# The first two weight tiles of each MLP, computed token-major in a four-layer hybrid trunk

## What is computed

```python
def rmsnorm(x, g):
    y = xf * lax.rsqrt(jnp.mean(xf * xf, axis=-1, keepdims=True) + NORM_EPS)
    return (y * g.astype(jnp.float32)).astype(x.dtype)

def sq_relu_mlp(h, w1, w2):
    a = jax.nn.relu(h @ w1)
    return (a * a) @ w2

x = x + sq_relu_mlp(rmsnorm(x, norm_mlp[i]), mlp_w1[i], mlp_w2[i])
```

## Time and profile before

| | |
|---|---|
| runs of before | 1424.39, 1426.0, 1428.05 us; median 1426.0 us |
| span of the profiled execution | 1423.9 us |
| PE busy | 1357.3 us, 95% of the span |
| DVE, ACT busy | 858.0 us (60%), 667.9 us (47%) |
| mean granted PE clock | 0.981 of full speed |
| DMA | 162 GB/s on average |

### The profile page before, as it was taken

How to read it: one execution, slowest core, us unless ns; L and a number is a source line. 1 busy time by engine, 2 the same in 40 slices (tenths; PEclk the granted TensorE clock), 3 DMA queues, 4 the chain that set the end, 5 groups by cost and what they waited for, 6 DMA issues and landing times.

```text
span 1423.9 us, 20299 instructions
## 1 busy us (share of the span) xinstructions
PE 1357.3 (95%) x8600; PEld 1212.8 (85%) x8600; DVE 858.0 (60%) x1125; ACT 667.9 (47%) x834; POOL 40.3 (3%) x58
## 2 busy tenths in 40 slices
PE   5999989999999899999998999999999999899997
PEld 5788779999899799998897988999988787799996
DVE  4676565555554565555897786655555766565553
ACT  3454444444354454443665554544434454454442
POOL 2000000000000000000101110000000000000000
PEclk9899999999999999999998999999998999999999
DMA  7653246655565275552773444665626143375540
GB/s 235 173 145 119 89 163 214 199 178 178 151 175 178 93 248 185 198 182 89 231 231 114 149 149 133 221 196 192 190 60 237 54 137 99 103 236 189 196 149 30
DMA packets 147834, 231.06 MB, mean 162 GB/s; under 512 B 7651, under 2 KB 116493, under 8 KB 147744
## 3 DMA queue, kind: packets, MB, share of 16 engines
q1 hardware_dynamic: 144896, 221.66, 47.5%
q0 software_dynamic: 2848, 8.10, 2.7%
HBM read 227.08 MB, written 2.65 MB: 161 GB/s over the span
## 4 chain that ended last, share of the span: by engine, by line
PE 85%; DVE 8%; ACT 3%; issue 2%; DMA 2%; POOL 0%; SPq 0%; DVEq 0%; POOLq 0%; ACTq 0%
PE bank L501 14%; PE bank L503 14%; PE bank L502 14%; PE acc L696 11%; PE acc L695 11%; PE acc L699 11%; PE bank L829 4%; DVE wlo L484 3%; ACT whi L474 2%; PE bank L847 1%; PE bank L837 1%; DMA raw<-in_mla_w_in 1%; PE bank L630 1%; DMA raw<-in_mla_w_ukv 1%; PE bank L1270 1%
## 5 line engine op out<-in xcount | busy, mean ns | idle before, releaser
L484 DVE TENSOR_TENSOR wlo<-raw,whi 128x2048 fp32r<-128x2048 f32 (+2 forms) x209 | 467.5, 2246 | 208.0 <-ACT whi L474 207.9
L474 ACT ACTIVATE whi<-raw 128x2048 fp32r<-128x2048 f32 (+2 forms) x209 | 388.7, 1870 | 94.1 <-PE acc L699 82.9
L501 PE MATMUL bank<-hhi,whi 128*128 128x256 f32 x1448 | 415.7, 287 | 11.1 <-DVE hlo L574 7.1
L502 PE MATMUL bank<-hlo,whi 128*128 128x256 f32 x1448 | 411.8, 284 | 0.0
L503 PE MATMUL bank<-hhi,wlo 128*128 128x256 f32 x1448 | 411.8, 284 | 0.0
L501 PEld LDWEIGHTS bank<-hhi,whi 128*128 128x128 f32 x1448 | 278.8, 193 | 17.3 <-DVE hlo L574 9.0
L502 PEld LDWEIGHTS bank<-hlo,whi 128*128 128x128 f32 x1448 | 279.0, 193 | 3.3 <-issue 1.0
L503 PEld LDWEIGHTS bank<-hhi,wlo 128*128 128x128 f32 x1448 | 278.9, 193 | 0.2
L696 PE MATMUL acc<-wlo,uhi 128*128 128x512 f32 x512 | 200.0, 391 | 0.0
L695 PE MATMUL acc<-whi,uhi 128*128 128x512 f32 x512 | 199.6, 390 | 0.0
L699 PE MATMUL acc<-whi,ulo 128*128 128x512 f32 x512 | 159.1, 389 | 0.0
(11 more groups left out here) (212 smaller groups left out, 1678.2 us busy)
## 6 DMA issues: line engine op xcount, KB each, us to landing
raw<-in_mlp_w SPq DMA_DIRECT2D x128, 1024.0 KB, 5.3
raw<-in_ssd_w_in SPq DMA_DIRECT2D x18, 1024.0 KB, 6.2
raw<-in_mla_w_o SPq DMA_DIRECT2D x16, 1024.0 KB, 4.9
raw<-in_mla_w_ukv SPq DMA_DIRECT2D x8, 1024.0 KB, 7.4
raw<-in_moba_w_qkv SPq DMA_DIRECT2D x16, 512.0 KB, 6.1
raw<-in_ssd_w_out SPq DMA_DIRECT2D x8, 1024.0 KB, 5.0
raw<-in_mla_w_uq SPq DMA_DIRECT2D x8, 768.0 KB, 6.4
raw<-in_mla_w_in SPq DMA_DIRECT2D x4, 1024.0 KB, 9.1
```

What stands on the lines that cost most here:

```text
L474: nc.scalar.activation(whi[:, s, :e], raw[:, s, :e], ACT.Copy).then_inc(w_hi_done[s], 1)
L484: nc.vector.tensor_tensor(wlo[:, s, :e], raw[:, s, :e], whi[:, s, :e].bitcast(F32), ALU.subtract).then_inc(w_split[s], 1)
L501: nc.tensor.matmul(ps, lhs[0], rhs[0], start=start, stop=False)
L502: nc.tensor.matmul(ps, lhs[0], rhs[1], start=False, stop=False)
```

## The change

The products of up 0 and up 1 are taken the other way round: the turned input of one token tile is stationary (128 tokens) and 256 weight columns move. The four pieces (token tile t, unit c) are `rows(t, c)`, 24 matmuls each, and the result of a tile, 128 tokens by 512 hidden channels, stands in one PSUM bank. Relu and square are taken in that layout. Then `turn(t)` turns the squares of a tile with four transposes into a bank, from which ACT and DVE make `uhi` and `ulo`. PE's order becomes rows(0,0), the eight transposes of tile 1, rows(0,1), rows(1,0), rows(1,1), turn(0), up 2, turn(1), down 0, down 1, up 3, down 2 and on as before. DVE scales both halves of tile 1 before it makes any of tile 1's `hlo`. ACT and DVE split up 2 between the two tiles' relus and squares, and down 1 between the two tiles' `uhi` and `ulo`.

```diff
@@ plan_mlp
+                if c == 1:
+                    jobs.add(("rows", L, 0))
+                    jobs.add(("rows", L, 1), ready=used(("up", L, 1)))
+                    jobs.add(("uT", L, 0), freed=(ulo_done, mlp_base[L] + 1))
+                elif 2 <= c < NCH:
                     jobs.add(("up", L, c), ready=used(("up", L, c)))
+                    if c == 2:
+                        jobs.add(("uT", L, 1), freed=(ulo_done, mlp_base[L] + 2))
@@ dve_norm, deferred
-                dve_tr(dve, j, 1, [0])
                 dve_scale_half(dve, j, 1, 1)
-                dve_tr(dve, j, 1, [1])
+                dve_tr(dve, j, 1)
@@ pe_mlp
             def down(c, tiles=range(T)):
-                te.wait_ge(ulo_done, mlp_base[L] + c + 1)
+                te.wait_ge(ulo_done, mlp_base[L] + max(c + 1, T))
                 pe_out(te, ("down", L, c), hidden(c), c == 0, False, tiles)

-            pe_first_channels(te, j, [("up", L, 0), ("up", L, 1)])
+            def rows(t, c):
+                wait_unit(te, ("up", L, c))
+                ps = open_job(te, ("rows", L, t)) if c == 0 else bank[jobs.at["rows", L, t][0]]
+                w = hi_lo(("up", L, c))
+                for k in range(KD):
+                    mm = mm3(ps[:, c * CH:(c + 1) * CH], (hhi[:, k, tok(t)], hlo[:, k, tok(t)]),
+                             (w[0][:, k, :], w[1][:, k, :]), k == 0, k == KD - 1)
+                if t == T - 1:
+                    mm.then_inc(used(("up", L, c))[0], 1)
+                elif c == 1:
+                    mm.then_inc(ready(("rows", L, t)), 1)
+
+            def turn(t):
+                te.wait_ge(usq_done, mlp_base[L] + t + 1)
+                ps = open_job(te, ("uT", L, t))
+                for b in range(4):
+                    mm = nc.tensor.transpose(ps[:, b * P:(b + 1) * P], rsq[:, t, b * P:(b + 1) * P], ident[:])
+                mm.then_inc(ready(("uT", L, t)), 1)
+
+            tile_ready(te, j, 0)
+            rows(0, 0)
+            pe_tr(te, j, 1)
+            rows(0, 1)
+            tile_ready(te, j, 1)
+            rows(1, 0)
+            rows(1, 1)
+            turn(0)
+            wait_unit(te, ("up", L, 2))
+            pe_channels(te, open_job(te, ("up", L, 2)), ("up", L, 2), CH)
+            turn(1)
             for c in range(2, NCH):
                 down(c - 2, [0] if c == NCH - 1 else range(T))
-                wait_unit(te, ("up", L, c))
-                pe_channels(te, open_job(te, ("up", L, c)), ("up", L, c), CH)
+                if c > 2:
+                    wait_unit(te, ("up", L, c))
+                    pe_channels(te, open_job(te, ("up", L, c)), ("up", L, c), CH)
@@ act_mlp
-            for c in range(NCH):
+            for t in range(T):
+                act_splits(act, ("up", L, 0), AHEAD - 1 + t)
+                ps = job_ready(act, ("rows", L, t))
+                nc.scalar.activation(relu[:, t, :], ps[:], ACT.Relu).then_inc(freed(("rows", L, t)), 1)
+            for t in range(T):
+                ps = job_ready(act, ("uT", L, t))
+                nc.scalar.activation(turned(uhi, t), ps[:].rearrange("p (b n) -> p b n", b=4),
+                                     ACT.Copy).then_inc(uhi_done, 1)
+                if t == 0:
+                    act_splits(act, ("down", L, 0), AHEAD - 1)
+            for c in range(2, NCH):
@@ dve_mlp
-            for c in range(NCH):
+            for t in range(T):
+                dve_splits(dve, ("up", L, 0), AHEAD - 1 + t)
+                job_copied(dve, ("rows", L, t))
+                nc.vector.tensor_tensor(rsq[:, t, :], relu[:, t, :], relu[:, t, :], ALU.mult).then_inc(usq_done, 1)
+            dve_square_rstd(dve, j)
+            for t in range(T):
+                dve.wait_ge(uhi_done, mlp_base[L] + t + 1)
+                nc.vector.tensor_tensor(turned(ulo, t), bank[jobs.at["uT", L, t][0]][:].rearrange("p (b n) -> p b n", b=4),
+                                        turned(uhi, t).bitcast(F32), ALU.subtract).then_inc(ulo_done, 1)
+                if t == 0:
+                    dve_splits(dve, ("down", L, 0), AHEAD - 1)
+            for c in range(2, NCH):
```

More of the change, by code:

```diff
@@ L294, in plan_mlp @@
                     unit(("up", L, c), KD, CH, cols(w1, c * CH, (c + 1) * CH))
+                if c == 1:
[3 more added lines that the diff above has]
+                elif 2 <= c < NCH:
                     jobs.add(("up", L, c), ready=used(("up", L, c)))
+                    if c == 2:
+                        jobs.add(("uT", L, 1), freed=(ulo_done, mlp_base[L] + 2))
                 if c >= 1:
                     unit(("down", L, c - 1), 2, DM, rows(w2, (c - 1) * CH, c * CH))
+        mlp_base, n_mlp = {}, 0
+        for kind, L, i in stages:
+            if kind == "mlp":
+                mlp_base[L] = NCH * n_mlp
+                n_mlp += 1
         step_unit = {}
@@ L766, in mlp_splits, with turned @@
         def mlp_splits(splits, eng, L, c):
[L768 to L771, removed]
+            splits(eng, ("down", L, c - 1), AHEAD - 1 if c < NCH - 1 else 1)
+        def turned(hidden, t):
+            return hidden[:, :, :, tok(t)].rearrange("p c i n -> p (c i) n")
         def act_mlp(act, j, L):
-            for c in range(NCH):
+            for t in range(T):
[9 more added lines that the diff above has]
+            for c in range(2, NCH):
                 mlp_splits(act_splits, act, L, c)
@@ L796, in dve_mlp @@
                                         ALU.subtract).then_inc(ulo_done, 1)
-                if c == 0:
-                    dve_square_rstd(dve, j)
             dve_splits(dve, ("down", L, NCH - 1), AHEAD - 1)
[L801 to L805, removed]
         def pe_attn(te, j, L, heads, qk, qk_waits, v_of, v_waits, piece):
```

## The result

The changed kernel took **1428.18 us** (median of 20 runs, 1424.23 to 1431.22), the one before 1424.51 us (20 runs beside them). The ratio is **1.0025, 95% interval 1.0016 to 1.0033**: 3.7 us slower, a difference that 20 runs each can show, and just under the 0.3% that the prediction took as its bound. One run of before beside experiments 1 to 4, 2227.2 us at a granted clock of 0.556, was in a slower state and is left out throughout.

What follows compares the result with a forecast made beforehand. PE, 85% of the span, bounds the kernel. Per MLP +0.88 +1.30 +1.67 -2.43, less 0.16, is +1.26 us, four times +5.0: span 1428.9, plus 2.1 to the runs' median, 1431.0 us; range 1427.0 to 1435.5.

Steps and rivals of the forecast that it cites:

- The saving at the front: At each MLP's entry, PE's old waits for tile 1's `xn` and `hlo` and small pieces go: 2.43 us saved per MLP.
- Turned operands at no cost: In up 0 and up 1, 96 matmuls of 256 columns before and after, still 0.12 us each with the weights moving.
- The transposes: turn(0) and turn(1) add eight transposes in PE's queue: 0.88 us per MLP, 3.5 us in all.
- The wait for up 2's weights: PE ahead of up 2 waits for DVE's split of its weights: 1.30 us per MLP, none before.
- The wait for `ulo`: Between turn(1) and down 0 PE waits for ACT's copy and DVE's rest: 2.03 us, 1.67 of it beside the transposes.
- The stretch: From the old stage's last matmul to the start of down 1: 27.3 us instead of 26.03, 1.26 us later per MLP.
- The clock: One fall of the granted clock still expected among the four MLP entries, as before, so 4 x 1.26 = +5.0 us.
- Rival (a): The third MLP's clock fall goes: +3.5, 1429.5 us; if the fourth's goes too, +2.0, 1428.0; chance 27 in 100.
- my own sum: The main forecast over four MLP entries: +5.0 us, 1431.0 us, its own range 1429.5 to 1432.5; 45 in 100.
- Rival (b): The clock falls two to four more times behind new idle with transposes, 1.5 us each: 1434.0 to 1437.0 us; chance 17.
- Rival (c): Not slower: DVE ends up 2's split by 201.01, so no wait there; 1425.8 us, or 1424.3; chance 7 in 100.
- Rival (d): PE still stands at tile 1's transposes or rows(1,0), old waits stay: +8.7 us more, 1439.7 us; chance 4 in 100.

Runs made afterwards that it cites:

- Experiment 1: Changed kernel with turn(1) placed between the two halves of up 2 instead of behind it; 1422.34 us, ratio to before 0.9986.
- experiment 2: Changed kernel with ACT's two sums of squares moved from ahead of down 0's split to behind up 2's split; 1424.77 us, ratio to before 1.0006.
- experiment 3: Changed kernel with turn(1) in the middle of up 2 and ACT's sums of squares behind up 2's split; 1416.01 us, ratio to before 0.9939.
- experiment 4: Changed kernel with each group of four transposes of squares issued twice, same values written twice; 1429.38 us, ratio to before 1.0026.
- Experiment 6: Changed kernel with DVE's old order, first half of tile 1's `hlo` ahead of scaling its second half; 1442.04 us, ratio to before 1.0133.
- experiment 7: Kernel before with only ACT's two sums of squares moved behind down 0's split; 1424.09 us, ratio to before 1.0003.
- experiment 5: Changed kernel with tile 1's eight transposes ahead of rows(0,0) instead of behind it; 1428.66 us, ratio to before 1.0031.

## Why the prediction was right

**The saving at the front: right.** 2.43 us of waits per MLP were to go, and no idle is left between the old stage's last matmul and turn(0). The two slacks claimed for `xn` and `hlo` were there: 1.26 us (`xn` scaled at 188.44, turned from 189.70) and about 1.1 (the second `hlo` done at 192.26, rows(1,0) due at 193.4). Experiment 6 shows that the first depends wholly on DVE's new order.

**Turned operands at no cost: right.** 72 matmuls in 8.7 us is 0.12 us each, as with the input moving.

**The transposes: right in price.** Eight more per MLP; four take 0.36 us, and 0.44 when something follows at once (experiment 4: 2.45 instead of 2.01 us). The figure of some 275 ns each, cited from the Trainium skill's "TensorE: Matmul & The Clock Gate" (Part 4: PE-mode transpose; there for bf16), agrees with the duration of this trace's float32 rows (median 273 ns), but that is not what a row of them takes.

**The wait for up 2's weights: right, a little over.** Forecast 1.30 us, measured 1.12 (1.48 less 0.36); the difference is ACT's two copies, which ended 1.72 us behind the start of the eight transposes (190.33 + 1.09 against 189.70) and not 1.90: the model for them, at tile 0, had a wait for `xn` inside. Its cause, the chain of sums, splits and first square, is shown by experiments 2 and 7.

**The wait for `ulo`: right.** Forecast 2.03 us from turn(1) to down 0, measured 2.01. Experiment 1 shows the cause. The matmul behind it takes 0.33 us to the next start instead of 0.23, which I had not counted.

**How well the sum fits is in part luck.** Up 2 started 0.18 us sooner behind turn(0) than forecast, but it took 5.85 us and down 0 5.59, not 5.75 and 5.47. These errors of 0.1 to 0.2 us cancel.

**The stretch: right.** Forecast 27.3 us, measured 27.31 to 27.33, so +1.28 us per MLP at full clock, 5.1 us in all.

**The clock: the term that was off.** I took the net fall of the third MLP as staying, at one among the four entries. In the changed kernel's trace none of the four stretches has one, nor has the 1.98 us idle ahead of the fourth. Rival (a) was right for this profile: with the measured windows, 109.27 us against 105.67, the entries are +3.6, and the 1.45 us ahead of the fourth MLP is gone as well. Over many runs the effect is smaller. The mean granted clock was 0.9811 in the 20 runs of the change and 0.9803 in the 47 of before beside the experiments, 27.0 and 28.0 us of the span lost if the whole of it is charged: -1.0, so 4.1 us. Against these 47 runs (median 1423.84) the change is 4.3 us slower, against its own 20 runs of before 3.7. If only runs with the same recorded clock are compared (five groups, 0.979 to 0.983, weighted by the change's runs), it is 4.7 us slower; single groups give 3.2 to 6.9. The clocks are rounded to 0.001 (1.4 us), so that the step from 5.1 to 3.7 is consistent with the clock and the spread of before, but not shown to be them.

**The starting point.** 1431.0 stood on a median of three runs, 1426.0; twenty gave 1424.51. Of the 2.8 us by which the forecast was too high, 1.5 come from there and 1.3 from the sum. So the measured 1428.18 lies outside the range of my own sum (1429.5 to 1432.5), and the +3.7 us outside what I held likelier than not, slower by over 4.3 us. That it lies 0.2 us from the 1428.0 of rival (a) is luck: as a difference (a) had +2.0.

**Rival (b), falls behind the new waits,** did not occur: four transposes followed by 1.41 us of idle (eight in experiment 4) stand in 20 entries of five profiled kernels (the change and experiments 2, 4, 5, 6), and none was followed by a fall. **Rival (c), up 2's weights in time,** would have needed the sums out of the way; experiment 2 made exactly this case, and gave its "no difference to before" (1.0006). Its stretch there is 26.2 us (20.58 to down 0 and 5.59 for it), against 26.03 before. **Rival (d)** did not occur; experiment 6, in which PE does stand at tile 1's transposes, shows what that costs: +8.7 us in the entries.

## What to carry to other kernels

To start with the part of the data that is ready removes a wait only if what follows has its own inputs in time. Here PE asked for up 2's weights 7.5 us earlier (12.75 us instead of 20.28 behind the old stage's last matmul), while ACT kept its two sums of squares ahead of the splits; moving these two sums and one group of transposes into the middle of independent work turned 3.7 us of loss into 7.6 us of gain. When a chain PE, ACT, DVE, PE is unavoidable, price it from a place where the same chain already runs, and ask which independent work can stand inside it.

## What the runs showed of the hardware

- **The clock falls behind idle of about 2 us, and not always.** 2.01 us between two groups of transposes was followed by a fall in two of four places (experiment 6), the single 1.98 us ahead of tile 0's transposes in 4 of 27 (three places in each of the nine traces that have it). Idle of 0.35 and 1.41 us with four transposes between was followed by one in the third MLP both in the kernel before and in experiment 7, and in none of their other three. Single idle of 1.41 us behind four or eight transposes was not, in 20 places. Each fall put PE at the lower level (1.2 GHz) and cost about 1.5 us where nothing hid it.
- **A fall can hide.** In experiment 6 the two MLPs with a fall had no wait for up 2's weights (up 2 0.36 us behind turn(0) instead of 1.43): ACT's sums of squares took 1.05 and 1.06 us and a DVE `hlo` 0.69 us inside the fall, as at full clock, so the splits lost nothing while PE came later. Down 0 came 24.31 and 24.30 us behind the old stage instead of 23.90 in the first MLP, 0.4 us and not 1.5.
- **The first matmul behind transposes or a wait takes longer to the next start**: 0.20 us instead of 0.12 behind transposes (190.49 to 190.69 in the changed kernel), 0.22 behind a wait of 0.88 us (200.69 to 200.91), 0.33 instead of 0.23 for 512 columns behind the wait for `ulo` (208.55 to 208.88).
